# Attention over pairs of heads in 25 steps, and state sums of both chunk halves issued alternately

## The reference

```
# linear attention, per chunk of 64 tokens: what a chunk adds to the state
ds = jnp.einsum("nbhsd,nbhsv->nbhdv", k_end, vc)
s' = dec * s + ds                       # scan over chunks, both directions

# windowed attention, per block of 128 queries of one head
s_ctx = q . k_ctx * scale               # 128 context keys
s_loc = q . kn * scale                  # 384 latent keys: the block before, its own, the one after
p = softmax(concat([s_ctx, s_loc, sink]))[..., :-1]
o = p[..., :P] . v_ctx + p[..., P:] . vn
# the context block reads only its own 128 keys
```

## Time and profile before

| | |
|---|---|
| median of 3 runs | 2179.14 us (2176.87 to 2185.44) |
| the profiled execution | 2180.98 us, its span 2178.9 us |
| mean granted TensorE clock | 0.931 of full |
| PE busy | 1892.1 us, 87% |
| PEld busy | 1653.2 us, 76% |
| DVE busy | 1116.9 us, 51% |
| ACT busy | 676.4 us, 31% |
| POOL busy | 626.5 us, 29% |
| chain that ended last | PE 71%, DVE 9%, ACT 6%, issue 6%, DMA 3% |
| moved by DMA | 325.90 MB, 150 GB/s on average |

### The profile page before, as it was taken

One profiled execution on the slowest core, in us unless ns is written; L12 is line 12 of the kernel. 1 busy time (PEld: TensorE's weight loads), 2 busy tenths in 40 slices (PEclk: granted clock), 3 DMA queues, 4 the chain that ended last, 5 costly groups with the idle time before them and its releaser, 6 DMA issues.

```text
span 2178.9 us, 31324 instructions
## 1 busy us (share of the span) xinstructions
PE 1892.1 (87%) x11778; PEld 1653.2 (76%) x11778; DVE 1116.9 (51%) x1533; ACT 676.4 (31%) x974; POOL 626.5 (29%) x421
## 2 busy tenths in 40 slices
PE   2799999999999988599629999999999999949991
PEld 0689999888898966477418999998889887737770
DVE  0526765544132244788582466654432332568885
ACT  1223331333200002477532332224330000127773
POOL 0343342222354540000034333432224444200001
PEclk8799999999999997799859999999999999959995
DMA  7322222111355464899762222211125456069984
GB/s 271 92 74 60 63 59 52 52 47 41 103 172 171 152 229 156 297 378 377 249 204 61 64 55 64 61 47 46 51 62 160 150 180 229 39 211 345 377 310 174
DMA packets 304192, 325.90 MB, mean 150 GB/s; under 512 B 48400, under 2 KB 246160, under 8 KB 304064
## 3 DMA queue, kind: packets, MB, share of 16 engines
q1 hardware_dynamic: 272032, 239.49, 35.4%
q10 hardware_dynamic: 24544, 57.39, 7.2%
q0 software_dynamic: 7488, 27.27, 3.3%
HBM read 290.17 MB, written 33.91 MB: 149 GB/s over the span
## 4 chain that ended last, share of the span: by engine, by line
PE 71%; DVE 9%; ACT 6%; issue 6%; DMA 3%; DVEq 2%; ACTq 1%; POOL 1%; POOLq 0%; SPq 0%; PEldq 0%
PE ps L1739 42%; PE ps L2178 5%; PE ps L1753 5%; ACT w_hi L1111 3%; PE ps L1989 3%; DVE w_lo L1652 2%; PE ps L1837 2%; PE ps L1769 2%; PE ps L2099 2%; DMA raw<-in_w_ada 2%; PE ps L2169 1%; ACT yo L1128 1%; PE ps L1980 1%; PE ps L1848 1%; PE ps L1858 1%
## 5 line engine op out<-in xcount | busy, mean ns | idle before, releaser
L725 POOL CAST w_hi<-raw 128x1024 fp32r<-128x1024 f32 (+2 forms) x180 | 178.6, 992 | 957.0 <-PE ps L1739 670.5
L1739 PE MATMUL ps<-hT_hi,w_hi 128*128 128x320 f32 (+1 forms) x1760 | 410.7, 314 | 7.6 <-DVE hT_lo L1198 4.7
L1739 PE MATMUL ps<-hT_lo,w_hi 128*128 128x320 f32 (+1 forms) x1760 | 403.2, 310 | 0.0
L1739 PE MATMUL ps<-hT_hi,w_lo 128*128 128x320 f32 (+1 forms) x1760 | 403.2, 310 | 0.0
L727 POOL TENSOR_TENSOR w_lo<-raw,w_hi 128x1024 fp32r<-128x1024 f32 (+2 forms) x180 | 390.6, 2170 | 37.6 <-issue 12.4
L1739 PEld LDWEIGHTS ps<-hT_hi,w_hi 128*128 128x128 f32 (+1 forms) x1760 | 293.4, 188 | 19.4 <-issue 10.9
L1739 PEld LDWEIGHTS ps<-hT_lo,w_hi 128*128 128x128 f32 (+1 forms) x1760 | 295.0, 188 | 1.1
L1739 PEld LDWEIGHTS ps<-hT_hi,w_lo 128*128 128x128 f32 (+1 forms) x1760 | 294.9, 188 | 1.1
L757 POOL DMA_INDIRECT xg<-h_scratch,sidx x32 | 31.2, 975 | 425.8 <-PE ps L2169 281.3
L2178 PE MATMUL ps<-w_hi,xT_hi 128*128 128x512 f32 x256 | 109.5, 428 | 40.2 <-DVE w_lo L1652 40.2
L1057 ACT ACTIVATE sg<-ps 128x640 f32<-128x640 f32 x32 | 22.5, 704 | 357.4 <-PE ps L1739 357.4
(11 more groups left out here) (269 smaller groups left out, 3336.4 us busy)
## 6 DMA issues: line engine op xcount, KB each, us to landing
raw<-in_w_in SPq DMA_DIRECT2D x108, 512.0 KB, 4.8
raw<-in_w_ada SPq DMA_DIRECT2D x96, 512.0 KB, 7.2
raw_more<-in_w_exp_down SPq DMA_DIRECT2D x72, 256.0 KB, 6.7
raw<-in_w_exp_gate SPq DMA_DIRECT2D x68, 256.0 KB, 5.9
raw<-in_w_exp_up SPq DMA_DIRECT2D x68, 256.0 KB, 7.7
expert_scratch<-yo ACTq DMA_DIRECT2D x32, 512.0 KB, 6.1
raw_more<-in_w_exp_gate SPq DMA_DIRECT2D x60, 256.0 KB, 5.9
raw_more<-in_w_exp_up SPq DMA_DIRECT2D x60, 256.0 KB, 7.7
```

The costliest lines, as they stand in the source:

```text
L725: nc.gpsimd.tensor_copy(hi[:, 0:n], raw[:, slot, 0:n])
L1739: ins = mm(ps[0:m, 2 * b + c, 0:HT], w[:, k * m:(k + 1) * m], act_pair[h][:, chunk0 + k, HT * c:HT * (c + 1)], start=(k == 0 and i == 0), ...
```

## The change

Three edits.

1. *State sums.* Even and odd chunks are issued alternately, one pair per token tile. Where each lands is given by a function `state_sum`: even and odd chunks always go to different banks (direction `d` to banks `2d` and `2d + 1`, the fifth tile of both directions to banks 4 and 5). The wait for `s_cc` stands after the four pairs of direction 0; both directions' fifth pairs follow, then the four pairs of direction 1. The wait of TensorE on `s_gds` between the halves is gone; `s_gds` is raised once per direction.
2. *Attention.* The 4 pairs of heads and 5 query blocks make steps `(p, b)`; the list `STEPS` has five more, `p = 4`, in which only the last pair's values are left: 25. In a step TensorE does `weigh` of the block before of pair `p - 1`, `turn` of block `b` of pair `p - 1`, `scores` of block `b` of pair `p`, and one dense unit where the table `DENSE` has one: none in the steps `(p, 3)`, and in the last five only `yA 7` in `(4, 1)`. Within `scores` and `weigh` the two heads' matmuls are issued alternately. Scores of both heads go to banks 0 and 1 (1 and 4 for the context block), turned probabilities to banks 2 and 3, of which ScalarE copies both at once. VectorE takes both heads' scores of a step, takes their maximum at once, and normalises the step before. ScalarE copies, then does the exponentials of a step. Nothing is double-buffered by block any more except by the pair that `s_sb` holds one step apart.
3. *Order and small things.* `ORDER` takes the dense units from `DENSE`, so their order changes a little. The eight memsets of masked score blocks are gone, since the maximum reads only the columns that exist; `nsink` holds the negated sinks; the sums of a step lie in `small`.

The diff, cut to its core:

```diff
+PAIRS = AH // KVH
+DENSE = {(0, 0): ("mA", 1), (0, 1): ("Q", 1), (0, 2): ("yA", 1), (0, 4): ("mA", 2),
+         (1, 0): ("yA", 2), (1, 1): ("Q", 2), (1, 2): ("mA", 3), (1, 4): ("yA", 3),
+         (2, 0): ("mA", 4), (2, 1): ("Q", 3), (2, 2): ("yA", 4), (2, 4): ("mA", 5),
+         (3, 0): ("yA", 5), (3, 1): ("mA", 6), (3, 2): ("yA", 6), (3, 4): ("mA", 7),
+         (4, 1): ("yA", 7)}
+STEPS = [(p, b) for p in range(PAIRS + 1) for b in range(TILES)]
+ORDER += [("Q", 0), ("mA", 0), ("yA", 0)] + [DENSE[s] for s in STEPS if s in DENSE]
...
+        def state_sum(d, n):
+            t, q = n // 2, n % 2
+            if t == PT:
+                return ps[:, 4 + q, d * DV:(d + 1) * DV]
+            return ps[:, 2 * d + q, t * DV:(t + 1) * DV]
...
+        def score_bank(i, b):
+            return ((0, 1), (1, 4))[b == PT][i]
...
+    def exps(p, b):
+        n = (l * PAIRS + p) * TILES + b
+        lo_, hi_ = span(b)
+        act.wait_ge(s_nm, SET + n + 1)
+        for i in range(KVH):
+            j, hd = KVH * b + i, HEAD_OF[KVH * p + i]
+            A(s_sb[:, i, b, lo_:hi_], s_sb[:, i, b, lo_:hi_], ACT.Exp, bias=a_nm[:, j:j + 1], accum_out=a_rs[:, j:j + 1])
+            ins = A(a_es[:, j:j + 1], a_nm[:, j:j + 1], ACT.Exp, bias=sink[:, hd:hd + 1])
+        ins.then_inc(s_ex, 1)
+
+    def probs_copy(p, b):
+        act.wait_ge(s_pt, SET + (l * PAIRS + p) * TILES + b + 1)
+        cols = ktiles(b) * P
+        nc.scalar.copy(pT[:, :, 0:cols], ps[:, 2:4, 0:cols]).then_inc(s_pte, 1)
...
+    stored = 0
+    for p, b in STEPS:
+        if p:
+            probs_copy(p - 1, b)
+        if p < PAIRS:
+            exps(p, b)
+        what, n = DENSE.get((p, b), ("", 0))
+        if stored < n and what != "Q":
+            store_a(stored)
+            stored += 1
+        if what == "mA":
+            gate_a(n)
+        elif what == "Q":
+            q_chunk(n)
+    while stored < KC:
+        store_a(stored)
+        stored += 1
...
+    def scores(p, b):
+        n = (l * PAIRS + p) * TILES + b
+        lo_, hi_ = span(b)
+        if p:
+            dve.wait_ge(s_pt, SET + n - TILES + 1)
+        dve.wait_ge(s_sc, SET + n + 1)
+        for i in range(KVH):
+            ins = V.scalar_tensor_tensor(s_sb[:, i, b, lo_:hi_], ps[:, score_bank(i, b), lo_:hi_], float(HD) ** -0.5, strip[:, lo_:hi_],
+                                         ALU.mult, ALU.add)
+        ins.then_inc(s_sce, 1)
+        dve.drain()
+        j = slice(KVH * b, KVH * b + KVH)
+        V.tensor_reduce(a_mx[:, j], s_sb[:, :, b, lo_:hi_], AX.X, ALU.max)
+        dve.drain()
+        V.scalar_tensor_tensor(a_nm[:, j], a_mx[:, j], -1.0, nsink[:, p::PAIRS], ALU.mult, ALU.min).then_inc(s_nm, 1)
...
+    for s, (p, b) in enumerate(STEPS):
+        if p < PAIRS:
+            scores(p, b)
+        if s and STEPS[s - 1][0] < PAIRS:
+            normalise(*STEPS[s - 1])
+        if b == 0 and p >= 2:
+            take_y(p - 2)
+        if b == PT and p + 1 < PAIRS:
+            rope(p + 2, qT[:, (p + 1) % 2, 0:SAMPLE])
+        what, n = DENSE.get((p, b), ("", 0))
+        if what == "yA":
+            branch_a(n)
+    take_y(PAIRS - 1)
...
     for d in range(2):
-        if d:
-            pe.wait_ge(s_cc, SET + hh + 1)
-        for q in range(2):
-            if q:
-                pe.wait_ge(s_gds, SET + hh * 4 + 2 * d + 1)
-                hold(pe)
-            o = CHUNK * q
-            for t in range(TILES):
-                n = 2 * t + q
-                ins = mm(psf[:, 1536 * d + n * DV:1536 * d + (n + 1) * DV], zb[o:o + CHUNK, d, t * P:(t + 1) * P],
-                         v_sb[o:o + CHUNK, h, t, :], start=True, stop=True)
-            ins.then_inc(s_gds, 1)
+        def both(d_, t):
+            for q in range(2):
+                o = CHUNK * q
+                ins_ = mm(state_sum(d_, 2 * t + q), zb[o:o + CHUNK, d_, t * P:(t + 1) * P],
+                          v_sb[o:o + CHUNK, h, t, :], start=True, stop=True)
+            return ins_
+        for t in range(PT):
+            ins = both(d, t)
+        if d == 0:
+            pe.wait_ge(s_cc, SET + hh + 1)
+            both(1, PT)
+            ins = both(0, PT)
+        ins.then_inc(s_gds, 1)
...
-            pe.wait_ge(s_sce, SET + (l * AH + 2 * j - 2) * TILES)
+            pe.wait_ge(s_sce, SET + (l * PAIRS + j - 2) * TILES + PT)
...
+    def scores(p, b):
+        n = (l * PAIRS + p) * TILES + b
+        if b == 0:
+            pe.wait_ge(s_rope, SET + l * 5 + p + 2)
+            pe.wait_ge(s_qc, SET + l * 4 + p + 1)
+            if p == 0:
+                pe.wait_ge(s_kc, SET + l + 1)
+        if b == PT and p >= 2:
+            pe.wait_ge(s_yc, SET + l * PAIRS + p - 1)
+        pe.wait_ge(s_sce, SET + n)
+        own_ = P + b * P
+        if b == PT:
+            parts = [(P, own_, P)]
+        elif b == 0:
+            parts = [(P, own_, P), (2 * P, 0, P), (3 * P, own_ + P, P)]
+        else:
+            parts = [(0, own_ - P, 2 * P), (2 * P, 0, P)] + ([(3 * P, own_ + P, P)] if b < PT - 1 else [])
+        for to, from_, m in parts:
+            for i in range(KVH):
+                rows = slice(HD * i, HD * (i + 1))
+                ins = mm(ps[:, score_bank(i, b), to:to + m], qT[rows, p % 2, b * P:(b + 1) * P], kT[rows, from_:from_ + m], start=True, stop=True)
+        ins.then_inc(s_sc, 1)
+    def turn(p, b):
+        n = (l * PAIRS + p) * TILES + b
+        lo_, hi_ = span(b)
+        pe.wait_ge(s_p, SET + n + 1)
+        pe.wait_ge(s_pte, SET + n)
+        if p == 0 and b == 0:
             pe.wait_ge(s_sigA, SET + l * KC + 1)
+        for j in range(ktiles(b)):
+            for i in range(KVH):
+                ins = tr(ps[:, 2 + i, j * P:(j + 1) * P], s_sb[:, i, b, lo_ + j * P:lo_ + (j + 1) * P], ident)
+        ins.then_inc(s_pt, 1)
+    def weigh(p, b):
+        n = (l * PAIRS + p) * TILES + b
+        pe.wait_ge(s_pte, SET + n + 1)
+        if b == 0 and p:
+            pe.wait_ge(s_yc, SET + l * PAIRS + p)
+        if b == PT and p + 1 < PAIRS:
+            pe.wait_ge(s_sce, SET + n + TILES + 1)
...
+        for j, v in enumerate(vals):
+            for i in range(KVH):
+                o = HD * i
+                dst = ps[o:o + HD, 4, 0:P] if b == PT else ps[o:o + HD, 5, b * P:(b + 1) * P]
+                ins = mm(dst, v[:, o:o + HD], pT[:, i, j * P:(j + 1) * P], start=(j == 0), stop=(j == len(vals) - 1))
+        if b == PT:
+            ins.then_inc(s_ao, 1)
...
+    last = ("yA", 0)
+    for p, b in STEPS:
+        q, c = (p - 1, b - 1) if b else (p - 2, PT)
+        if q >= 0:
+            weigh(q, c)
+        if p:
+            turn(p - 1, b)
+        if p < PAIRS:
+            if b == PT and p + 1 < PAIRS:
+                rotate(p + 2)
+            scores(p, b)
+        if (p, b) in DENSE:
+            what, n = DENSE[p, b]
+            if last[0] == "Q":
+                pe.wait_ge(s_kraw, SET + l * 5 + last[1] + 2)
+            elif last[0] == "mA":
+                pe.wait_ge(s_sigA, SET + l * KC + last[1] + 1)
+            else:
+                pe.wait_ge(s_zA, SET + l * KC + last[1] + 1)
+            {"mA": gate_a, "yA": branch_a, "Q": q_chunk}[what](n)
+            last = what, n
+    weigh(PAIRS - 1, PT)
```

More of the change, by code:

```diff
@@ L231, in build @@
         b_rt = own("b_rt", [P, NG + NE])
-        small = own("small", [P, 80])
+        small = own("small", [P, 88])
         tri_b = own("tri_b", [P, 2 * P], BF16)
@@ L375, in build @@
         g_ss, g_ln, g_rs = small[:, 15:20], small[:, 20:25], small[:, 25:30]
-        a_mx, a_rd = small[:, 30:35], small[:, 35:40]
-        a_nm, a_rs, a_es = ([small[:, 40 + 10 * i + 5 * j:45 + 10 * i + 5 * j] for j in range(2)] for i in range(3))
+        a_mx, a_rd, a_nm, a_rs, a_es = (small[:, 30 + 10 * i:40 + 10 * i] for i in range(5))
+        nsink = small[:, 80:88]
         ps = ctx.enter_context(nc.psum_tensor("ps", [P, 8, 512], F32))
@@ L1384, in rope @@
                     V.tensor_tensor(dst, rt1[:, :], rt2[:, :], ALU.add).then_inc(s_rope, 1)
-                def scores(i):
-                    b_ = l * AH + i
-                    if i >= 2:
-                        dve.wait_ge(s_pt, SET + (b_ - 1) * TILES)
-                    for b in range(TILES):
-                        lo_, hi_ = span(b)
-                        dve.wait_ge(s_sc, SET + b_ * TILES + b + 1)
-                        V.scalar_tensor_tensor(s_sb[:, i % 2, b, lo_:hi_], ps[:, b % 2, lo_:hi_], float(HD) ** -0.5, strip[:, lo_:hi_],
-                                               ALU.mult, ALU.add).then_inc(s_sce, 1)
@@ L1407, in normalise @@
+                def normalise(p, b):
+                    lo_, hi_ = span(b)
+                    j = slice(KVH * b, KVH * b + KVH)
+                    dve.wait_ge(s_ex, SET + (l * PAIRS + p) * TILES + b + 1)
+                    V.tensor_tensor(a_rd[:, j], a_rs[:, j], a_es[:, j], ALU.add)
                     dve.drain()
-                    V.reciprocal(a_rd, a_rd)
+                    V.reciprocal(a_rd[:, j], a_rd[:, j])
```

(6 more changed lines are left out.)

213 lines of the change are left out of this document (10 added, 203 removed).

## The result

| | before | after |
|---|---|---|
| median, us (4 runs each, same chip) | 2181.41 | 2107.82 |
| lowest to highest | 2176.87 to 2185.44 | 2102.31 to 2116.25 |
| ratio after to before, 95% | | 0.9662 (0.9643 to 0.968) |
| profiled execution, us (span) | 2180.98 (2178.9) | 2102.31 (2100.5) |

The change takes 73.6 us off the median. The forecast was 2102 within 2084 to 2135. The profiled execution of after is the lowest of its four.

A forecast was written before the change was run, and what follows sets the result against it. TensorE was taken to bound the attention stage. From 2180.98 us, 21 for state sums and 57 for the two stages came off, giving 2103, or 2101 against the median; forecast 2102, own range 2088 to 2118, wider range 2084 to 2135.

The forecast's parts named there:

- state sums, per head: State sums of 8 heads: 5.08 us each falls to 2.45 by alternating halves, 21 us saved in all.
- do two halves share fully: Matmuls on opposite row or column halves of TensorE run at once, taken at the full factor two.
- stage, per layer: Attention stage, first score matmul to first merge unit: 189.8 us falls to 161.5, saving 57 us over both layers.
- TensorE work in it: Attention stage of one layer: dense units, scores, value products, turns, rotations and shape changes sum to 149.7 us.
- waits in it: New TensorE waits on VectorE and ScalarE in one layer's attention stage: 9.3 us, bounds 4 and 20.
- clock at the start: Start of the attention stage: the 0.68 average clock goes, since dense work mA1 covers VectorE's lateness.
- clock in or behind the tail: Last steps of the attention stage: low clock may return among waits and short blocks, 2.5 us taken, 5.1 at most.
- state steps of VectorE: VectorE's state steps after the state sums would end at 166, still covered by dense work by 1 us.
- (2,0): Attention step: TensorE waits 0.5 us for rotary work queued on VectorE, with only 3.5 us of dense cover.
- Half the packing gain: Scores and state sums: row halves overlap less than column halves; 2144 us in full, about 2123 for half; chance 0.12.
- The finer pipeline waiting in every step: Attention stages: VectorE or ScalarE meets each of 50 steps 0.5 us late; +25 us, 2127; chance 0.14.
- The clock through the stage: Attention stages: turns and short blocks keep TensorE at the lower clock; +130 to 150 us a layer, 2380; chance 0.04.

The follow-up runs named there:

- Experiment 1: The kernel before with only the state sums changed to alternating halves; 2160.9 us, ratio 0.9888 to before.
- experiment 2: The kernel after, but within a step one head's score matmuls are all issued before the other's; 2122.56 us, ratio 0.9718 to before.
- experiment 3: The kernel after, but within a step one head's value matmuls are all issued before the other's; 2118.02 us, ratio 0.9689 to before.
- experiment 4: The kernel after, but each direction's first four tiles of state sums issue even chunks first, then odd; 2117.99 us, ratio 0.9694 to before.
- experiment 8: The kernel after, but state sums and value products alternate in groups of two fp32 matmuls; 2112.95 us, ratio 0.9677 to before.
- experiment 9: The kernel after with pair 0's four pieces of dense work each one step later; 2111.41 us, ratio 0.9671 to before.
- experiment 10: The kernel after with pair 0's dense work begun two steps later, three score blocks in a row first; 2113.79 us, ratio 0.9687 to before.
- experiment 11: The kernel after with second banks and copy buffer for the last pair's odd blocks, earlier turns, yA7 behind the last value product; 2093.47 us.
- experiment 6: The kernel after with only yA7 moved from step (4,1) to behind the last value product; 2109.21 us, ratio 0.9665 to before.
- experiment 12: The kernel after with second banks and copy buffer for the last pair's odd blocks, earlier turns, yA7 left in place; 2103.89 us.
- experiment 7: The kernel after with dense units dealt out anew to cover the tail, leaving long runs of steps without any; 2121.6 us, ratio 0.9726 to before.
- its control: The kernel after run again unchanged, as the measure for later runs; 2108.64 us, ratio 0.9673 to before.

## Why the prediction was right, point by point

| step of the prediction | predicted | measured |
|---|---|---|
| state sums, per head | 2.45 us, saved 2.6 | 2.43, saved 2.65 |
| do two halves share fully | factor 2 | 16 value records 1.03 us where 8 took 1.02 |
| stage, per layer | 161.5 us | 161.92, 162.31 |
| TensorE work in it | 149.7 | 151.5 busy |
| waits in it | 9.3 (its list adds up to 9.6) | 10.4 idle |
| clock at the start | back to 1.00 | 1.00 |
| clock in or behind the tail | 2.5 us lost in the stage | 1.6 lost, in the first merge unit behind it |
| state steps of VectorE | covered by 1 us | covered by 1.2 us |

- *Overlap.* This decided the forecast, and it was right for the reason given: the earlier trace rows showed concurrency in both directions of the array, and the new blocks have it in full. Experiment 1 shows it for row halves over 40 records. The factors that the Trainium skill gives ("TensorE: Matmul & The Clock Gate", Part 3: Packing small matmuls, the measured speedups: 3.07 for four row tiles, 2.38 for three column tiles) would have put two tiles at about 1.55 to 1.6, as an estimate. No run here has three or four tiles; for two the measurement decides, and it is 2. The same part's formula, one matmul's duration plus about 4 ns for each further tile, would add at most 0.03 us for 8 pairs (an estimate); the trace agrees, with 16 value records of two heads 0.01 us longer than 8 of one.
- *That it needs the alternation* the prediction took for granted. It is so for about half of the gain: a block by head keeps the overlap of four records at the seam (experiments 2 to 4, 8).
- *Waits.* (0,4) 1.4 us, predicted 1.3. (3,1) 1.5, predicted 1.5. The tail: 1.24, 1.10, 0.89, 0.46 and 2.00 before the merge, predicted 1.15, 1.15, 0.9, 0.5 and 2.0. The one that was mis-sized is (2,0), the rotary work queued on VectorE: predicted 0.5, measured 1.6 (the row with `qT` above). The 3 x 0.2 for the steps without a dense unit did not show. The places are right because each step was worked out from what stands ahead in VectorE's queue. In the work, the rotations were put too low: 1.7 us for three, where one takes 1.03 (437.59 to 438.62, change of shape included).
- *Where the number was lucky.* Work and waits of the stage came out 2.9 us above the prediction's 159.0, and the 2.5 us of low clock that it put into the stage did not come there; the two make 161.9 look like the forecast's 161.5. In the whole span the slow first merge units (3.2 us) were hidden by the scatter of 5 us behind the second stage. The overlap, the cost of the blocks and the places of the waits are not luck.
- *The start's clock.* The fall went, as said. The reason given, that dense work behind the first score block covers VectorE's lateness, is not what does it: with two such covers removed the clock still stays at 1.00 (experiments 9, 10), and before the change the clock fell 2.2 us ahead of the wait of 0.88 us. The outcome was right there and the reason was not; what did lower it before stays open.
- *The tail's clock.* Predicted at 2.5 us within the stage, measured 1.6 behind it. The fall follows 10.16 us in which TensorE is busy 5.71. Where the waits are removed (experiment 11, 8.19 us with 7.82 busy) it does not come, nor where only the last wait of 2.00 us is covered and the others stay (experiment 6). Where that one stays and the others are all but gone (experiment 12) it comes in the second layer and not in the first.
- *Rivals.* Half the packing gain: refuted by 2.43 and 1.03 us. The finer pipeline waiting in every step: eight waits in 25 steps; it is real where dense work is dealt out worse (experiment 7, 13 us). The clock through the stage: 1.00 with turns in 20 of the 25 steps. The Trainium skill ("TensorE: Matmul & The Clock Gate", Part 4: PE-mode transpose) says that transposes don't bring on the full clock, since they don't count as work like other matmuls; here 1.0 us of turns stands in a step beside 2.1 us of products and mostly 3.6 or 7.2 of dense work, and the level holds, so the trace doesn't bear that rival out. No run here has turns alone.

Not settled is why single falls of the clock of 3.4 us come inside the stage in some executions: experiment 2 has one in either layer, 4, 6, 8, 11 and 12 have one or two in one of the layers, after and its control none. Each of them begins within 1.5 us behind the wait of 1.6 us at (2,0) or that of 1.5 to 1.9 us at (3,1), which after has as well and passes at 1.00. Those of experiment 7 stand in or behind its own waits of 1.8 us and more.

## What to carry to other kernels

Where matmuls use half of the array's rows or columns, issue those of the two halves in turn, or at least in groups of two; the second half was then free here, and the price of a block that of its longer half. When the packed engine stops being late, the next losses are short serial chains without other work, as in a pipeline's last steps: give the last steps a second buffer and keep one piece of independent work for the very end; here the large gain came from both together. And deal independent work out so that the slower side engine (here VectorE, 4.2 us a step) gets it behind each of its long queues.

## What the runs showed of the hardware

- Two streams on opposite halves of the rows (state sums, scores) or columns (value products) overlap in full: 40 records in 2.43 us instead of 5.08, two waits of 0.31 us among them.
- Without alternation the overlap reaches over the last four records of the first stream: 16 records in 1.51 us against 1.02 alternated; 40 sums in 3.19, in groups of two 2.53.
- The clock fell behind a 10.16 us tail in which TensorE was busy 5.71, not behind one of 8.19 with 7.82 busy, nor behind 11.08 us with 7.53 busy whose last wait of 2.0 us was covered. Three packed score blocks with two waits of 1.1 and 1.4 us did not lower it at all.
- Scores of one half at a time, before the change, went with a fall of the clock 4.9 us after their start, with one wait of 0.38 us ahead of it, in both layers (5.8 us after it in experiment 1), for 10.2 us. Eight blocks of state sums of 5.08 us, one half at a time too, stood between dense units at 1.00.
- The same code had falls of 3.4 us in one layer and none in the other (experiments 6 and 4: two in the second layer, none in the first), each right behind a wait of TensorE of 1.6 to 1.9 us, and the stretch behind the second stage scattered by 7 us. So a few us between two such kernels are not the change's.
